# Half-tile row sums, an early second expert tile, gate products a tile behind their one-hots, and 342 dense columns

## The reference, cut to what matters

```python
qry = (xt @ w_query).reshape(TOKEN_BLOCK, PEER_HEADS, 2, PEER_HALF)
v1, i1 = lax.top_k(s1, PEER_TOPK)            # 16 of 128 keys, for each of 8 heads
v2, i2 = lax.top_k(s2, PEER_TOPK)
top_s, pos = lax.top_k(cand, PEER_TOPK)      # 16 of 256 sums
idx = jnp.take_along_axis(cand_idx, pos, axis=-1)
gate = jax.nn.softmax(top_s, axis=-1)
pre = jnp.einsum('td,thkd->thk', xt, expert_down[idx])
act = jax.nn.gelu(pre, approximate=False) * gate
out = jnp.einsum('thk,thkd->td', act, expert_up[idx])
```

## Time and profile before

| | |
|---|---|
| Time, median of 3 runs | 3568.76 us (3567.64 to 3570.26) |
| Profiled execution: own time, span | 3564.6 us, 3562.8 us |
| Instructions | 50874 |
| PE busy | 3507.9 us (98%) |
| PEld busy | 3183.2 us (89%) |
| DVE busy | 2171.1 us (61%) |
| ACT busy | 1413.8 us (40%) |
| POOL busy | 2045.6 us (57%) |
| DMA | 895.04 MB, mean 251 GB/s |
| Up-side matmuls | 2564.1 to 3559.4 |

### The profile page before, as it was taken

How to read it: one execution, slowest core, us unless ns; L and a number is a source line. 1 busy time by engine, 2 the same in 40 slices (tenths; PEclk the granted TensorE clock), 3 DMA queues, 4 the chain that set the end, 5 groups by cost and what they waited for, 6 DMA issues and landing times.

```text
span 3562.8 us, 50874 instructions
## 1 busy us (share of the span) xinstructions
PE 3507.9 (98%) x20053; PEld 3183.2 (89%) x20053; DVE 2171.1 (61%) x3773; ACT 1413.8 (40%) x1780; POOL 2045.6 (57%) x718
## 2 busy tenths in 40 slices
PE   7999999999999999999999999999999999999999
PEld 5777777777788888898999999999999999999999
DVE  6333434343685137897676767443577777777774
ACT  5544545555422223323444444433333333333332
POOL 2333333333344434377666667687777777777774
PEclk9999999999999999999999999999999999999999
DMA  4322222222344332288999898999999999999994
GB/s 153 134 105 101 94 88 96 83 99 85 119 142 180 119 114 95 92 312 347 346 364 350 345 366 348 355 380 385 379 375 370 361 373 365 387 371 366 370 368 167
DMA packets 184738, 895.04 MB, mean 251 GB/s; under 512 B 15720, under 2 KB 69224, under 8 KB 90600
## 3 DMA queue, kind: packets, MB, share of 16 engines
q1 hardware_dynamic: 59232, 399.47, 30.1%
q0 software_dynamic: 49392, 359.68, 25.5%
q10 hardware_dynamic: 75928, 133.30, 10.2%
HBM read 828.39 MB, written 69.21 MB: 252 GB/s over the span
## 4 chain that ended last, share of the span: by engine, by line
PE 59%; issue 22%; DVE 8%; POOL 6%; DMA 3%; ACT 1%; DVEq 0%; ACTq 0%; POOLq 0%; SPq 0%
PE ps L1524 56%; DVE ps L1309 6%; POOL w_lo L350 5%; PE ps L1754 2%; DMA expert_rows<-down_rows,idx 1%; DVE h_dense L1442 1%; DMA w_e_raw<-w_stream 1%; POOL w_e_lo L357 1%; DVE expert_rows L1296 0%; PE ps L1688 0%; DMA g_dram<-gate_buf 0%; DVE hn_lo L1139 0%; POOL expert_rows L385 0%; ACTq L847 0%; ACT w_e_hi L724 0%
## 5 line engine op out<-in xcount | busy, mean ns | idle before, releaser
L357 POOL TENSOR_TENSOR w_e_lo<-w_e_raw,w_e_hi 128x2048 fp32r<-128x2048 f32 x256 | 1184.5, 4628 | 476.4 <-ACT w_e_hi L724 474.9
L350 POOL TENSOR_TENSOR w_lo<-w_raw,w_hi 128x2048 fp32r<-128x2048 f32 x115 | 536.6, 4666 | 934.2 <-ACT w_hi L417 934.2
L1524 PE MATMUL ps<-sn_hi,w_e_hi 128*128 128x344 f32 x2048 | 664.2, 324 | 11.4 <-POOL w_e_lo L357 8.7
L1524 PE MATMUL ps<-act_hi,w_e_hi 128*128 128x344 f32 x2048 | 658.4, 321 | 11.4 <-DVE h_dense L1442 11.4
L1524 PE MATMUL ps<-sn_lo,w_e_hi 128*128 128x344 f32 x2048 | 655.3, 320 | 0.0
L1524 PE MATMUL ps<-act_hi,w_e_lo 128*128 128x344 f32 x2048 | 655.2, 320 | 0.0
L1524 PE MATMUL ps<-sn_hi,w_e_lo 128*128 128x344 f32 x2048 | 654.1, 319 | 0.0
L1524 PE MATMUL ps<-act_lo,w_e_hi 128*128 128x344 f32 x2048 | 651.5, 318 | 0.0
L724 ACT ACTIVATE w_e_hi<-w_e_raw 128x2048 fp32r<-128x2048 f32 x256 | 489.2, 1911 | 191.3 <-DMA w_e_raw<-w_stream 106.6
L1296 DVE SCALAR_TENSOR_TENSOR expert_rows<-expert_rows,ps 128x2048 f32<-128x2048 f32 x171 | 388.3, 2282 | 259.7 <-DMA expert_rows<-down_rows,idx 143.2
L1524 PE MATMUL ps<-xn_hi,w_hi 128*128 128x512 f32 x1088 | 447.2, 411 | 18.7 <-DVE xn_lo L927 18.7
(11 more groups left out here) (260 smaller groups left out, 4853.7 us busy)
## 6 DMA issues: line engine op xcount, KB each, us to landing
w_e_raw<-w_stream SPq DMA_DIRECT2D x256, 1024.0 KB
w_raw<-w_stream SPq DMA_DIRECT2D x116, 1024.0 KB, 4.8
gel_dram<-gel_all ACTq DMA_DIRECT2D x32, 704.0 KB
g_dram<-gate_buf ACTq DMA_DIRECT2D x11, 2048.0 KB
gel_in<-gel_dram ACTq DMA_DIRECT2D x32, 704.0 KB
g_exp<-g_dram ACTq DMA_DIRECT2D x32, 704.0 KB
gate_dram<-g_raw ACTq DMA_DIRECT2D x32, 256.0 KB, 2.0
g_in<-gate_dram ACTq DMA_DIRECT2D x16, 512.0 KB, 5.8
```

The lines of the kernel that those rows point to most:

```text
L350: nc.gpsimd.tensor_tensor(wlo[s][:, :], raw[s][:, :], whi[s][:, :].bitcast(F32), ALU.subtract).then_inc(lo_ready, 1)
L357: nc.gpsimd.tensor_tensor(e_lo[j % 4][:, :], e_raw[j % 4][:, :], e_hi[j % 3][:, :].bitcast(F32), ALU.subtract).then_inc(lo_ready, 1)
L1524: m = mm(ps[:, bank, 0:width], lhs[:, w], r, start=(n % (3 * per) == 0), stop=(n % (3 * per) == 3 * per - 1))
```

## The change

Five things are changed. **Width.** 42 extra tokens for 40: the dense width of every expert matmul is 342 for 344, still three copies (126 partitions), still 43 row sets and 86 quartets. **Rows.** `ITEM_HALF` gives each row a half tile; DVE sums the first half's row and the second half's apart. **Second expert tile.** ACT makes the high part of tile 1 right behind that of tile 0, and the last query goes out after 9 pieces of sn_hi; POOL waits for all of sn_lo before the low part of tile 1 and not after that of tile 2. **Gates.** PE's products and ACT's copies of quartet n are a tile later, the one-hots where they were. **Early gathers.** `FIRST_USED` is later by 1, 1, 2, 2, 3 and 3 tiles.

```diff
-XT = 40
+XT = 42
-N_GATES = TD // 4
+N_GATES = -(-TD // 4)
-FIRST_USED = [5, 9, 11, 14, 16, 18]
+FIRST_USED = [6, 10, 13, 16, 19, 21]
-ITEM_TILE = [T_GATES + (i - FIRST_ROWS) * DOT_TILES // (ADD_X - FIRST_ROWS) if i < ADD_X
-             else T_ACT + 1 + (i - ADD_X) * ADD_TILES // (N_ITEMS - ADD_X)
+ITEM_HALF = [2 * T_GATES + (i - FIRST_ROWS) * 2 * DOT_TILES // (ADD_X - FIRST_ROWS) if i < ADD_X
+             else 2 * T_ACT + 2 + (i - ADD_X) * 2 * ADD_TILES // (N_ITEMS - ADD_X)
              for i in range(FIRST_ROWS, N_ITEMS)]
+ITEM_TILE = [k // 2 for k in ITEM_HALF]
...
             for t in range(2 * EXPERT_TILES):
+                if t == 0:
+                    pool.wait_ge(slo_ready, CT)
                 if t + 1 < 2 * EXPERT_TILES:
                     low(t + 1)
                 if t == 1:
                     pool.wait_ge(idx3_ready, 1)
-                    pool.wait_ge(slo_ready, CT)
...
                         peer_hi(0)
+                        peer_hi(1)
...
             key_out(CT - 2)
-            peer_hi(1)
             for c in range(CT):
                 scaled_hi(c)
-            query_out(CT - 1, 1)
+                if c == CT // 2:
+                    query_out(CT - 1, 1)
             key_out(CT - 1)
...
-                    if GATE_TILE[n] == t:
+                    if GATE_TILE[n] + 1 == t:
                         gates_out(n)
...
                         one_hots(n)
+                rows_of_half(2 * t)
                 k = t - T_FIRST - 3
...
                 if t == T_ACT:
                     sparse_acts()
-                rows_of_tile(t)
+                rows_of_half(2 * t + 1)
...
+                for q in range(4):
+                    add_dense(g, 4 * q)
+                    if g + 1 < GROUPS:
+                        product(n + q, q)
+                    add_dense(g, 4 * q + 1)
+                    rows_of_half(2 * (t + q))
+                    add_dense(g, 4 * q + 2)
+                    if g + 1 < GROUPS:
+                        low(n + q, s, q)
+                    add_dense(g, 4 * q + 3)
+                    rows_of_half(2 * (t + q) + 1)
...
                 extras = {12 + 24 * k: [lambda n=n: gates(n)]
-                          for k, n in enumerate(n for n in range(N_GATES) if GATE_TILE[n] == t)}
+                          for k, n in enumerate(n for n in range(N_GATES) if GATE_TILE[n] + 1 == t)}
```

More of the change, by code:

```diff
@@ L196, in build @@
         tv_sum, tv_rec = at("tv_sum", 206.5, 32), at("tv_rec", 206.625, 32)
-        gt = at("gt", 187, TD)
-        i1_t, i2_t = at("i1_t", 199, TD), at("i2_t", 201, TD)
+        gt = at("gt", 187, 4 * N_GATES)
+        i1_t, i2_t = at("i1_t", 199, 4 * N_GATES), at("i2_t", 201, 4 * N_GATES)
         gel_in = [at("gel_in0", 181, 4 * W), at("gel_in1", 117, 4 * W)]
@@ L823, in _ @@
                     act.wait_ge(tk_tr, 1)
-                    nc.scalar.activation(gt[:, :], ps[:, GB, 0:TD], ACT.Copy).then_inc(gthi_ready, 1)
+                    nc.scalar.activation(gt[:, :], ps[:, GB, 0:4 * N_GATES], ACT.Copy).then_inc(gthi_ready, 1)
                 if T_FIRST + 3 < t <= T_FIRST + 7:
@@ L1310, in add_row, with rows_of_half @@
                                              op0=ALU.mult, op1=ALU.add).then_inc(row_used, 1)
-            def rows_of_tile(t):
+            def rows_of_half(k):
                 for i in range(FIRST_ROWS, N_ITEMS):
-                    if tile_of(i) == t and i != TURN_X:
+                    if ITEM_HALF[i - FIRST_ROWS] == k and i != TURN_X:
                         if i < ADD_X:
@@ L1377, in _ @@
             v.wait_ge(tk_tr, 3)
-            vec.tensor_copy(i1_t[:, :], ps[:, GB + 1, 0:TD])
-            vec.tensor_copy(i2_t[:, :], ps[:, GB, 0:TD]).then_inc(idx_ready, 1)
+            vec.tensor_copy(i1_t[:, :], ps[:, GB + 1, 0:4 * N_GATES])
+            vec.tensor_copy(i2_t[:, :], ps[:, GB, 0:4 * N_GATES]).then_inc(idx_ready, 1)
             v.wait_ge(gthi_ready, 1)
```

## The result

After: 3596.32 us, median of 4 runs (3593.83 to 3602.6), beside 3568.2 (3563.04 to 3570.26) of the kernel before in the same comparison: ratio 1.0085, 95% interval 1.0069 to 1.0101. Slower, as forecast, but by 28 us and not by 8, and above the upper end of the range. The profiled execution took 3596.49 us (span 3594.7), 31.9 more than that of before; its mean granted clock is 0.991, before 0.997.

The account below looks back on a forecast made before the run. PE was taken as busy throughout, with POOL's request list setting the pace between tiles 10 and 20. 4 + 8 + 18.3 - 4.2 + 0.7 - 18.5 = +8.3 us on 3564.6 profiled, so median 3577, range 3558 to 3590.

Parts of the forecast that it names:

- Width: Expert matmuls at 342 columns instead of 344: 0.83 ns less each, -5.1 us up side, -4.2 us down side from tile 22.
- a rival at 0.08: Expert matmuls on both sides: two columns bring nothing, +9.3 us, 3586; chance 0.08.
- The estimate from the Trainium skill: Expert matmuls: 0.13 ns a column, so the width would bring 3.2 us over both sides, not 10.2; set aside for the trace.
- Start of the down side: First two expert tiles: POOL begins tile 1's low part at 1499.5, and tile 1 starts at 1504.5, 6.1 us earlier.
- Tile 16: Down side: later requests for its rows give back the 6.1 us; it starts 4 us later (bounds -4.5 and +4.5).
- Tile 17: Down side: rows 16 to 19 requested behind two low parts; PE waits 7.0 us for the softmax, +8 with half clock.
- the first gate: PE's gate place in tile 21: rows 20 to 23 requested late, PE waits 18.9 us; +18.3 us (wait at least 11).
- The rest of the down side: +0.7 us without width: earlier one-hots -1.3, one of three gate stores finding no slack +2 (0 to +4).
- The up side: -18.5 us: row halves -22.4, 22 waits for low parts at group boundaries +9.0 (0 to +11), width -5.1.
- The rival on the other side: Late gathers don't hold the first gate; rows 20 to 23 used by 1681.6, -20.4 us, 3557; chance 0.12.
- The last rival: Batches land later and gate stores collide: the upper bounds and 4 us at the first gate, 3584; chance 0.15.
- the third: Rival for expert matmuls: two columns bring nothing, +9.3 us, 3586; chance 0.08.

Follow-up runs that it names:

- e15: Changed kernel with only the first four entries of the new `FIRST_USED`, the last two as before: 3576.47 us, ratio 1.0040 to the kernel before.
- e16: Changed kernel with only the last two entries of the new `FIRST_USED`, the first four as before: 3571.75 us, ratio 1.0025 to the kernel before.
- e4: Kernel before with its gate inserts a tile behind their one-hots, nothing else changed: 3567.04 us, ratio 1.0007.
- e5: Kernel before with its row sums by half tiles alone, at 344 columns with the old list: 3553.52 us, ratio 0.9969.
- e9: Changed kernel with the old list and, in a group's last tile, DVE's low part ahead of the row: 3549.26 us, ratio 0.9965 to the kernel before.
- e1: Changed kernel with the `FIRST_USED` list of the kernel before, everything else as changed: 3555.69 us, ratio 0.9984 to the kernel before.
- e7: Kernel before with down-side matmul widths stepped from 344 to 304 columns over tiles 93 to 110, rows 344 apart: 156.9 ns at 338, 153.9 at 336.
- e17: Changed kernel with the load of h_sparse and fold issued in the third tile of up-side group 16: 3592.96 us, ratio 1.0078 to the kernel before.
- e14: Changed kernel with the load of h_sparse and fold behind the loads of group 18: 3593.92 us, ratio 1.0093 to the kernel before.
- e13: Changed kernel with old list, gate places and 40 extra tokens, last low part first, exponential a tile later, h_sparse load behind group 18's: 3527.8 us, 0.9908.

## Why the prediction was wrong, step by step

The direction and the mechanism of the loss were right; the sum was 23.6 us too low in the profiled executions, and four terms were mis-sized.

**Width, 9.3 us of it.** -4.2 and -5.1 were forecast, 0 came; the forecast's bound "nothing, if width counts in steps of 8" came true as far as the nothing goes (the steps aren't shown). It was a rival at 0.08 because no row excluded either; the step that failed is the use of a slope over 168 columns for two. The estimate from the Trainium skill (TensorE: Matmul & The Clock Gate, Back-to-back issue gap), 0.13 ns a column, does not hold here either: 0 from 344 to 338, 0.45 on average below 336.

**Start of the down side: right.** Tile 1 at 1504.30 against 1504.5, behind the low part that starts at 1499.63 against 1499.5.

**Tile 16, 4.3 us.** Forecast +4, measured +8.3, by the mechanism named. Rows 12 to 15 were asked for at 1605.86 and not at 1602.2, since the tile whose low part stands ahead of them on POOL had itself landed late (1587.48 + 11.59). The last of them landed at 1626.60 and not 1619.1, 20.7 us after the first request where 16.9 was taken. Together that is 7.5 us, of which the forecast had kept some 3 for a gelu store. The step that failed is a landing measured in one batch and carried to another. Why this one took longer isn't settled: the DMA engines were busy for 0.80 of 1605 to 1627 (317 GB/s), against 0.92 (357 GB/s) in 1578 to 1600 of the kernel before, so it was not more traffic on the whole; from 1622 on they moved only 128 GB/s.

**Tile 17, 1.6 us more; the first gate, 0.9 less.** Waits of 8.2 and 17.7 against 7.0 and 18.9. At the gate the last row landed 15.4 us after the first request (1687.56 to 1702.95), where 17 was taken. e15 and e16 confirm which entry makes which.

**The rest of the down side, 4.1 us beside the width.** One gate store finding no slack was the right count, at the wrong price: forecast +2, while the wait of 4.1 us with its half clock makes 5.7 between tiles 80 and 86, as in e4 alone (4.9), and the gate product moved from before tile 22 adds 0.9, less what the waits that have gone give. A gate store takes 17.5 us on the chain, not 14.8.

**The up side, 5.3 us beside the width.** The forecast of -22.4 and +9.0 was nearly right (e5's up side: -12.3 in the trace, against -13.4), and e9 shows the cause of the second. What was missed is the stall at group 17: 2.7 us, another of 1.0 us and the clock, 3.5 in all from group 16 to 18 beside e1. The gates' load is issued later than before, 2.6 us ahead of group 16's first add where it was 6.5, but that doesn't explain the stall: it is 2.6 in e1, e5 and e15 too, where PE doesn't wait, and 5.1 in e9, where it does.

The rival on the other side, that the late gathers don't hold the first gate, is out: 17.7 us there. The last rival, batches landing later and gate stores colliding, happened in part: at tile 16, beyond its bound of 4.5, and at one gate store, but not at the first gate, where it had 4 us. Its number together with that of the third (two columns bring nothing) gives 3593, near the measured 3596 partly by luck, since its parts are off both ways. Still, rivals that exclude one another in a list of chances need not do so on the chip, and the range had no room for two of them at once.

## What to carry to other kernels

Where several engines follow one list by tiles, a request moved later in the list costs in full once its data's user is on the way to PE: price it from request to landing, by the spread of several such batches and not by one (15.4 to 20.7 us here). Take a gain per column only after a matmul at that width has been seen. When half of an edit gains and half loses, run the parts alone: here the row halves and the early start were hidden under the 36 us of a list. With the last low part ahead of the row they are worth 25 us together, and a kernel 37 us under the one before came from them, with a later exponential and one transfer moved; what these last two bring lies within the scatter of the medians.

## What the runs showed of the hardware

The spacing of these matmuls doesn't change between 344 and 338 columns (156.4 to 157.1 ns) and falls by 3.0 ns at 336 (e7). A DMA issue that takes 0.33 us on ACT (e17) held it for 12.44 us right behind a load of 704 KB in small pieces on the same queue (e14), with nothing but "issue" in the list of waits to show it; in e13, at the same place in the list, it held it for 5.51.
